# Hybrid SSD, pooling and MoE layer: adaLN modulation product as four 32-column TensorE groups

## What is computed

```python
ada = silu(cvec) @ w_ada + b_ada                 # 1024 -> 6144
shift1, scale1, gate1, shift2, scale2, gate2 = split(ada, 6)
h = rmsnorm(x, norm1_w) * (1 + scale1) + shift1
z, xBC, dt_raw, v = split(h @ w_in, ...)         # 1024 -> 1024, 1536, 32, 1024
xBC = silu(depthwise_conv(xBC))                  # then two SSD scans (need dt), pooling of v
mix = concat([rmsnorm(y * silu(z)), pooled]) @ w_out
x = x + gate1 * mix
h2 = rmsnorm(x, norm2_w) * (1 + scale2) + shift2
x = x + gate2 * routed_moe(h2)                   # 16 experts, top 2, float32
```

## Time and profile before

| | us |
|---|---|
| median of 3 runs (lowest, highest) | 1075.14 (1074.26, 1076.0) |
| profiled execution: its span, first to last instruction | 1072.6 |
| PE busy | 972.5 (91%) |
| DVE busy | 453.7 (42%) |
| POOL busy | 256.6 (24%) |
| ACT busy | 172.4 (16%) |
| L486 PE matmul, x640 records | 180.8, mean 441 ns |
| L467 PE matmul, x64 records | 30.3, mean 639 ns |
| L1274 DVE, the page's largest group x42 (of two) | 43.7 |

### The profile page before, as it was taken

How to read it: one execution, slowest core, us unless ns; L and a number is a source line. 1 busy time by engine, 2 the same in 40 slices (tenths; PEclk the granted TensorE clock), 3 DMA queues, 4 the chain that set the end, 5 groups by cost and what they waited for, 6 DMA issues and landing times.

```text
span 1072.6 us, 12656 instructions
## 1 busy us (share of the span) xinstructions
PE 972.5 (91%) x4829; PEld 619.7 (58%) x4829; DVE 453.7 (42%) x703; ACT 172.4 (16%) x354; POOL 256.6 (24%) x256
## 2 busy tenths in 40 slices
PE   6996969999899999999999969999999999999920
PEld 1444424555555555544444437888778887788800
DVE  0293997754674799854324460111111111111128
ACT  1511001211222222210001100110101011101123
POOL 0076999940142332300000000000000000000043
PEclk9998989999999999999999978999999999999965
DMA  9751452261310000474000058999999999989552
GB/s 345 305 196 40 156 212 104 79 236 59 118 39 1 1 1 1 180 273 177 16 4 20 22 215 321 330 340 328 333 324 329 350 328 332 323 320 351 209 201 112
DMA packets 34115, 204.60 MB, mean 191 GB/s; under 512 B 3730, under 2 KB 6290, under 8 KB 16291
## 3 DMA queue, kind: packets, MB, share of 16 engines
q1 hardware_dynamic: 22612, 168.42, 43.0%
q0 software_dynamic: 5472, 20.45, 5.1%
q10 hardware_dynamic: 6000, 15.31, 3.7%
HBM read 184.22 MB, written 19.96 MB: 190 GB/s over the span
## 4 chain that ended last, share of the span: by engine, by line
PE 59%; DVE 10%; issue 1%; DMA 1%; POOL 1%; ACT 1%; ACTq 0%; POOLq 0%; DVEq 0%
PE bank L839 23%; PE bank L717 12%; PE bank L851 11%; PE bank L581 6%; PE bank L823 2%; DVE ex L1405 1%; PE bank L619 1%; DVE xs L1458 1%; DVE ex L1687 1%; POOL ex L1200 1%; DVE ex L1421 1%; PE bank L683 1%; PE bank L770 1%; DVE uT L1704 1%; DMA ex<-slot_out,ri 1%
## 5 line engine op out<-in xcount | busy, mean ns | idle before, releaser
L839 PEld LDWEIGHTS bank<-yT,ex 128*128 128x128 f32 x2176 | 246.9, 193 | 9.0 <-issue 9.0
L839 PE MATMUL bank<-yT,ex 128*128 128x128 f32 x2176 | 247.2, 276 | 1.0 <-DVE yT L1665 1.0
L486 PE MATMUL bank<-hT,ring 128*128 128x512 f32 (+1 forms) x640 | 180.8, 441 | 0.4 <-ACT hT L885 0.4
L486 PEld LDWEIGHTS bank<-hT,ring 128*128 128x128 f32 x640 | 96.5, 194 | 75.3 <-issue 74.6
L851 PE MATMUL bank<-ex,yT 128*128 128x512 f32 x272 | 120.9, 597 | 0.0
L1672 DVE TENSOR_TENSOR yT<-yT,bank 128x128 f32<-128x128 f32 x68 | 19.5, 287 | 222.9 <-ACT yT L1061 222.9
L851 PEld LDWEIGHTS bank<-ex,yT 128*128 128x128 f32 x272 | 50.3, 190 | 57.8 <-issue 56.9
L581 PE MATMUL bank<-ring,hT 128*128 128x512 f32 x160 | 75.2, 604 | 4.5 <-DVE ex L1429 2.2
L1209 POOL DMA_INDIRECT yT<-h_dram,idx x17 | 17.2, 1011 | 252.4 <-PE bank L823 252.4
L717 PE MATMUL bank<-ring,yT 128*128 128x512 f32 x160 | 70.2, 593 | 0.8 <-DVE yT L1467 0.8
L1200 POOL TENSOR_TENSOR ex<-ex,dts 128x512 f32<-128x512 f32 x40 | 44.2, 1106 | 99.9 <-ACT ex L985 99.8
(11 more groups left out here) (267 smaller groups left out, 1122.7 us busy)
## 6 DMA issues: line engine op xcount, KB each, us to landing
ex<-w_exp SPq DMA_DIRECT2D x102, 1024.0 KB, 6.9
ring<-w_ring SPq DMA_DIRECT2D x12, 2048.0 KB, 9.4
yT<-w_late SPq DMA_DIRECT2D x12, 1024.0 KB, 4.9
slot_out<-yT ACTq DMA_DIRECT2D x17, 512.0 KB, 8.4
slot_out<-ex POOLq DMA_DIRECT2D x9, 512.0 KB, 6.7
ring<-w_ring SPq DMA_DIRECT2D x4, 1024.0 KB, 8.8
ex<-w_ring SPq DMA_DIRECT2D x2, 2048.0 KB, 9.9
ex<-x SPq DMA_DIRECT2D x5, 512.0 KB, 9.7
```

What stands on the lines that cost most here:

```text
L486: mm = pe.matmul(o, w[:, k, (f % 4) * P:(f % 4 + 1) * P], hT[:, k, lo:hi], start=(k == 0), stop=(k == KT - 1))
L839: mm = pe.matmul(psb[c % 2][:, a * P:(a + 1) * P], w[:, a, k, :], xgT[:, k, :], start=(k == 0), stop=(k == KT - 1))
```

## The change

`silc` becomes 32 columns per feature tile, two live and thirty zero. A weight chunk of 512 columns is multiplied as four matmuls of 128 columns, each with the same `silc` tile as stationary operand and each into its own 32 partitions of one PSUM bank (`ada_product`). All twelve chunks go this way: three from `ring`, the fourth from `adaw`, and eight late ones (gate2 among them) at f = 3 to 10. DVE's `ada_half` and PE's `gate2` go. The dt projection puts feature tile k into column group k % 4, and a matmul with a stacked identity (`C_STACK`) adds the groups while it turns them. x is turned without modulation, read out by plain copies, and modulated in place in `hT` by DVE. SP's order of loads changes with it.

```diff
-            def load_ring(n):
...
+            def load_ring(m):
+                if m >= RING:
+                    sp.wait_ge(s_used, m - 2 if m < 6 else m - 1)
+                sp.dma_start(ring[:, m % RING, :], w_ring[m if m < 3 else m + 1]).then_inc(s_ring[m % RING], 16)
+            for n in range(2):
+                load_ring(n)
+            for j in range(NJ):
+                sp.dma_start(xt[:, j, :], x[j * P:(j + 1) * P, :]).then_inc(s_x[j], 16)
+            load_ring(2)
+            for i in range(2):
+                sp.dma_start(adaw[i], w_ring[3, :, i * 2048:(i + 1) * 2048].rearrange("p (k c) -> p k c", k=4)).then_inc(
+                    s_adaw[i], 16)
             sp.dma_start(bcst, bconsts).then_inc(s_bconst, 16)
             sp.dma_start(wdt, w_dt).then_inc(s_wdt, 16)
+            load_ring(3)
...
+                if u == 0:
+                    sp.wait_ge(s_used, 4)
                 if u >= 2:
-                    sp.wait_ge(s_acc, u - 1)
+                    sp.wait_ge(s_adu, u - 1)
...
-            sp.wait_ge(s_op, 2)
-            for i in range(2):
-                sp.dma_start(w_g2[i], w_ring[NCH + 1 + i]).then_inc(s_g2w[i], 16)
-            sp.wait_ge(s_h2, NJ)
-            for c in range(6):
...
+            for c in (2, 3, 4, 5, 0, 1):
+                if c == 0:
+                    sp.wait_ge(s_h2, NJ)
                 sp.dma_start(ex[:, c * 2048:(c + 1) * 2048], w_exp[0, c]).then_inc(s_w_in[c], 16)
...
+            def ada_product(o, w, k, start, stop):
+                for g in range(AG):
+                    mm = pe.matmul(o[g * AR:(g + 1) * AR, 0:P], silc[:, k, :], w[:, g * P:(g + 1) * P],
+                                   start=start, stop=stop)
+                return mm
+            def ada_late(q):
+                if q == 0:
+                    pe.wait_ge(s_dif, 1)
+                if q >= 2:
+                    pe.wait_ge(s_adr, q - 1)
+                for h in range(2):
+                    pe.wait_ge(s_adaw[h], 16 * (q + 2))
+                    for kk in range(4):
+                        k = 4 * h + kk
+                        mm = ada_product(psb[q % 2], adaw[h][:, kk, :], k, k == 0, k == KT - 1)
+                    mm.then_inc(s_adu, 1)
+            for n in range(3):
+                ada_first(n)
             for j in range(NJ):
                 pe.wait_ge(s_xn, j + 1)
...
+            ada_first(3)
+            pe.wait_ge(s_arc, 4)
+            for n in range(4):
+                mm = pe.transpose(psb[0][:, n * P:(n + 1) * P], arow[:, n * P:(n + 1) * P], ident)
...
-                    for lo, hi, o in ((0, CTX, psb[1][0:32, 0:CTX]), (CTX, TOK, psb[0][0:32, :])):
-                        for k in range(KT):
+                    for k in range(KT):
+                        r = slice((k % AG) * AR, (k % AG + 1) * AR)
+                        for lo, hi, o in ((0, CTX, psb[1][r, 0:CTX]), (CTX, TOK, psb[0][r, :])):
...
-                if f in ADA_SUMS:
...
+                if f in ADA_AT:
+                    ada_late(ADA_AT.index(f))
...
-            gate2(0, range(0, 6))
             turn_h2(NJ - 1)
             router(NJ - 1)
-            gate2(0, range(6, KT))
-            gate2(1, range(0, 4))
...
-                act.activation(hT[:, k, CTX:TOK], psb[6 - 2 * (k % 2)][:, :], ACT.Identity,
-                               bias=modB[:, 2 * k + 1:2 * k + 2], scale=modA[:, 2 * k + 1:2 * k + 2]).then_inc(s_hs, 1)
+                act.activation(hT[:, k, CTX:TOK], psb[6 - 2 * (k % 2)][:, :], ACT.Copy).then_inc(s_hl, 1)
...
+            for n in range(3):
+                ada_row(n)
             dve.wait_ge(s_rs, 1)
...
+            for k in range(KT):
+                dve.wait_ge(s_xtr, k + 1)
+                dve.tensor_copy(hT[:, k, 0:CTX], psb[7 - 2 * (k % 2)][:, 0:CTX]).then_inc(s_hc, 1)
+            ada_row(3)
...
             for k in range(KT):
+                dve.wait_ge(s_hl, k + 1)
+                for c, lo, hi in ((0, 0, CTX), (1, CTX, TOK)):
+                    i = 2 * k + c
+                    ins = ts(hT[:, k, lo:hi], hT[:, k, lo:hi], modA[:, i:i + 1], modB[:, i:i + 1], ALU.mult, ALU.add)
+                ins.then_inc(s_hs, 1)
...
-                dve.wait_ge(s_ada, q + 1)
+                dve.wait_ge(s_adu, 2 * (q + 1))
```

More of the change, by code:

```diff
@@ L276, in trunk_kernel @@
         s_yT = sem("ssd_outputs_ready")
-        s_ads = [sem(f"ada_rows_{i}_stored") for i in range(2)]
+        s_ads = sem("ada_rows_stored")
         s_rowl = sem("ada_rows_loaded")
@@ L457, in _, with ada_first @@
             pe.wait_ge(s_const, 48)
-            for n in range(4):
-                if n in (1, 2):
+            def ada_product(o, w, k, start, stop):
[3 more added lines that the diff above has]
+                return mm
+            def ada_first(n):
+                if n < 3:
                     pe.wait_ge(s_ring[n], 16)
-                w = ring[:, n % RING, :].rearrange("p (k c) -> p k c", k=KT)
@@ L464, in _ @@
                 for k in range(KT):
-                    if n in (0, 3) and k % 4 == 0:
-                        pe.wait_ge(s_ring[0] if k else s_half, 32 if n else 16)
-                    mm = pe.matmul(psb[n][0:2, :], silc[:, 2 * k:2 * k + 2], w[:, k, :],
-                                   start=(k == 0), stop=(k == KT - 1))
+                    if n == 3 and k % 4 == 0:
+                        pe.wait_ge(s_adaw[k // 4], 16)
+                    w = adaw[k // 4][:, k % 4, :] if n == 3 else ring[:, n, k * 512:(k + 1) * 512]
@@ L555, in _ @@
                     pe.matmul(psb[0][:, 160:320], ones, a_, start=True, stop=True).then_inc(s_cum, 1)
-                if f in ADA_SUMS:
-                    q = ADA_SUMS.index(f)
-                    pe.wait_ge(s_acc, 2 * (q + 1))
-                    if q == 0:
-                        pe.wait_ge(s_dif, 1)
-                    else:
-                        pe.wait_ge(s_adr, q)
-                    for c in range(2):
-                        mm = pe.matmul(psb[c][0:1, :], ones[:, 0:1],
-                                       acc[q % 2][:, c * 512:(c + 1) * 512], start=True, stop=True)
-                    mm.then_inc(s_ada, 1)
+                if f in ADA_AT:
+                    ada_late(ADA_AT.index(f))
                 if f == 11:
@@ L807, in _ @@
             mm.then_inc(s_rk, 1)
-            gate2(1, range(4, KT))
             pe.wait_ge(s_pos, 1)
@@ L940, in _ @@
             act.wait_ge(s_tok, 10)
-            for i in range(2):
-                act.wait_ge(s_ads[i], 96)
+            act.wait_ge(s_ads, 32 * AG)
             for d in range(2):
@@ L1734, in layout @@
     cst[:, C_POS:C_POS + P] = p
+    cst[:, C_STACK:C_STACK + 32] = p[:, None] % 32 == np.arange(32)
     bc = np.zeros((P, B_ALL), f)
```

262 lines of the change are left out of this document (91 added, 171 removed).

## The result

The changed kernel takes 1057.83 us, median of 4 runs (1056.61 to 1061.04), against 1075.57 for the kernel before beside it: a ratio of 0.984, 95% interval 0.982 to 0.987, or 17.7 us less. A second series, beside the last experiments, gave 1059.60 and 0.985 (0.983 to 0.988). The forecast was 1077, no change; the rival with four groups at a time said 1057. The profiled execution is the slowest of the first series (1061.04), so its span is read for where time lies, and the medians for how much.

A forecast was written before the change was run, and what follows sets the result against it. PE was taken as the chain in the feature stage, waiting only on DVE. Head +9.2, feature stage -8.9 and routing +2.4 made +2.7 us on the median 1075.14, 1077.8, stated as 1077, a wash; range 1052 to 1097.

The forecast's parts named there:

- the rival with four groups at a time: Modulation chunks: all four column groups overlap, 1.9 us a chunk; -17.9 us, 1057 in all; chance 0.34.
- The chunk: One 512-column modulation product in four groups: two records run at a time, 3.8 us with waits (ends 1.9 and 7.2).
- dt: The dt projection in the feature stage, alternating column groups: 5.8 us instead of 8.80 (ends 2.2 and 8.8).
- +2.7: Whole kernel: sum of head +9.2, feature stage -8.9 and routing +2.4 us.
- The rest of the feature stage: Features 8.85 us each, dt's turn 1.1, decay sums 2.2 plus 0.3, softplus wait 0.4; reloads hidden.
- no wait at L558: Decay sums, feature stage: a small softplus-chain wait stays, 0.4 us, or nothing if DVE's instructions shorten.
- The head: Up to feature 0's end: later table, turns and fourth chunk end it at 64.6 instead of 55.34, 9.2 us later.
- The sentence that the table's wait hides nothing: Head: lifting that wait alone gains little; the third chunk's 33 low-clock records take 7.3 us, norm again at 41.
- Routing: Turn of h2 and router product at the low clock after idle: 1.94 and 3.6 us, 2.4 us more.
- The four cases: Column-group overlap: two at a time 0.38, four 0.34, none 0.15 (1111 us), partly 0.13 (1062 to 1100).
- two at a time: Modulation chunks and dt: the forecast's main case, two records running together, 3.8 us a chunk; chance 0.38.
- the forecast's own case: Whole kernel with two records at a time: 1077 us, own range 1070 to 1085.

The follow-up runs named there:

- the last experiments: Changed kernel with the head reordered and unread products in routing's four gaps, 1039.24 us (0.966); and the changed kernel repeated beside it, 1059.60 us.
- Lifting the wait: Changed kernel with the load of table bcst issued directly behind the 4 KB row, ahead of the ring: 1055.91 us (0.982).
- the filled gaps: Changed kernel with products that nothing reads in routing's four gaps: 6, 6, 7 and 6 gave 1056.07 us (0.983); 6, 6, 8 and 3 gave 1054.22 (0.979).
- four small moves: Changed kernel's head reordered: table early, x before second ring chunk, turns before third chunk's product, norm behind first row copy: 1045.93 us (0.974).
- runs of 4: Changed kernel, late chunks reordered to 2, 4, 8 or 16 successive records per column group: 1.9, 1.95, 4.23, 5.89 us a chunk.

## Why the prediction was wrong, point by point

- **The chunk: the step that failed.** "If PE starts records in the order of the program, the next group's first record can start no earlier than this group's second: two records run at a time." The "if" does not hold. PE takes records in that order, but a group keeps three waiting beside the one that runs, and records of the other groups start ahead of them: four start within 0.04 us where the program has two of each group in a row. So the second record of a float32 matmul holds up nobody. The term was 3.8 us and measured 1.88. The rival had the mechanism ("each group might hold one waiting record"; it is three), and the point held against it, that records would have to start out of order, is what they do. The Trainium skill (TensorE: Matmul & The Clock Gate, Part 3, The mechanism) has matmuls start and end strictly in program order; the starts measured here do not agree, and the measurement decides. The Trainium skill's sentence in the same section that weight loads overlap running matmuls only where the row group differs does not hold here: all groups share all 128 rows, and 64 loads of 0.11 us with their products fit into 1.88 us. The Trainium skill (TensorEngine Tiling (Array Packing), Key Properties) has different tiles load and multiply in parallel; the 0.0294 us a record agrees.
- **dt**, by the same assumption: 5.8 forecast, 2.33 measured (the lower end 2.2). Nine chunks on the path (eight late, one in the head) at 1.9 and dt at 3.5 make 20.6 us; +2.7 less that is -17.9, the rival's sum.
- **The rest of the feature stage held.** Feature 8.85, decay sums with what follows 2.61 (2.5), turn of dt 1.03 (1.1), and no wait at L558 (0.4, "nothing if DVE's instructions shorten"). No reload of a half was waited for, and no DVE wait took the place of the two removed. The stage is 119.3; with four groups 118.8 was said.
- **The head held but for the chunk.** The table's cast starts at 35.13 (landing at 35.7 was said), the norm ends at 42.07 (41.3; the 1.28 us of ACT's table load, which start when POOL is done, stand in no term), the turns take 7.3 (8.3), the chain behind the product 2.6 (2.3); feature 0 ends at 62.90 (64.6, or 62.65 with four groups). The sentence that the table's wait hides nothing, since the third chunk's product ends late anyway, failed with the chunk: 33 records at the low clock were to take 7.3 us, and took 3.6. Lifting the wait moved the norm by 5.8 us. That only 2.0 of it reached the end of the stage in that trace has a reason that the prediction didn't name, the clock in two features behind, which can fall there without the move too.
- **Routing held**: turn 1.97 (1.94), router 3.60 (3.6), together 2.5 more (2.4); the filled gaps show that the clock was the cause.
- **The chances.** The four cases were the right ones. Weight went to two at a time on an argument that no row of before could test, and the rival's 0.34 was close to its 0.38; the order between them was a guess about the depth of a queue. The range, 1052 to 1097, holds the 1057.83 because the rival's case was let into it; the forecast's own case ended at 1070. Two terms that no case had, +3.3 us in the scans and +0.4 behind routing, are in the trace.

## What to carry to other kernels

A product with few output rows that DVE accumulates can go to TensorE in four column groups at almost a quarter of the serial price, as long as the order of the program changes group at least every four records (two float32 matmuls); from there on the price climbs to 5.9 us for 1.9. When an engine is relieved, look at what its work kept busy: here the gate2 product had held up PE's clock in routing. After moving loads, walk the head again: four small moves there were worth two thirds of the whole change. And before a slow stretch is put down to an edit, see whether the unedited program has it in another execution.

## What was not expected of the hardware

- A column group holds three waiting float32 records besides the running one; a fourth stops everything behind it (1.95 us at runs of 4, 4.23 at 8). Records of other groups start ahead of those that wait (four within 0.04 us).
- The time saved ahead of a stage can vanish in the clock: 5.8 us at the turns became 2.0 at the end of the stage in one trace, while 14.6 of 14.6 stayed in another. Which it is need not be the edit's doing: of four executions with the same program up to routing, three have feature 0 in 8.89 us and one in 10.57.
- The column of the granted clock doesn't show a slow stretch at the very start. The first chunk of the changed kernel takes 3.64 us, 421 ns a record, at a shown clock of 1.00; the second 1.95 us and 274 ns at the same 1.00; the third 3.64 us at 0.51. The clock record kept with that trace begins at 16.2 us, where the first chunk ends, and the column reads 1.00 ahead of it. There the length of like records is the sign to go by.
